# A hybrid attention layer on one core: the softmax division of chunked attention moved to the last stage

## What is computed

```python
def chunk_relbias_attention(q, k, v, rel_bias):
    ...
    scores = scores + bias[None, None]
    ...
    probs = jax.nn.softmax(scores, axis=-1).astype(v.dtype)
    out = jnp.einsum('bnhqk,bnkhd->bnqhd', probs, vb)
...
    ya = ya * jax.nn.silu(ag)
    ...
    mix = jnp.concatenate([ya, yb], axis=-1) @ w_out[i]
    h = DN_ALPHA * x + mix
    h = h + jax.nn.sigmoid(h @ w_ple_gate[i]) * (p[i] @ w_ple_proj[i])
    x = layer_norm(h, ln_g[i], ln_b[i])
```

## Time and profile before

| | us |
|---|---|
| median of 3 runs | 2842.0 |
| lowest and highest | 2839.82, 2842.2 |
| span of the profiled execution | 2843.8 |
| TensorE busy | 2692.4 (95%) |
| VectorE busy | 1398.1 (49%) |
| ScalarE busy | 1192.5 (42%) |
| GpSimd busy | 336.2 (12%) |

### The profile page before, as it was taken

How to read it: one execution, slowest core, us unless ns; L and a number is a source line. 1 busy time by engine, 2 the same in 40 slices (tenths; PEclk the granted TensorE clock), 3 DMA queues, 4 the chain that set the end, 5 groups by cost and what they waited for, 6 DMA issues and landing times.

```text
span 2843.8 us, 40981 instructions
## 1 busy us (share of the span) xinstructions
PE 2692.4 (95%) x14544; PEld 2325.9 (82%) x14544; DVE 1398.1 (49%) x3367; ACT 1192.5 (42%) x2448; POOL 336.2 (12%) x227
## 2 busy tenths in 40 slices
PE   7999999999999999889989898987799999999997
PEld 5888888988888889878888888887688888888886
DVE  5211156232111461589989996778433334333343
ACT  3111122231111221589989997778322222222222
POOL 2000000000000000011111111334112221122211
PEclk9999999999999999999999997778899999999999
DMA  6431246453312463887767647785422211222111
GB/s 196 161 120 63 77 100 148 151 193 126 122 63 77 99 146 111 202 188 160 163 146 161 154 101 163 184 196 145 128 73 72 72 59 61 72 72 72 57 62 54
DMA packets 279246, 339.32 MB, mean 119 GB/s; under 512 B 81712, under 2 KB 201536, under 8 KB 274880
## 3 DMA queue, kind: packets, MB, share of 16 engines
q1 hardware_dynamic: 277648, 335.67, 43.8%
q0 software_dynamic: 1456, 1.86, 0.2%
HBM read 211.10 MB, written 127.41 MB: 119 GB/s over the span
## 4 chain that ended last, share of the span: by engine, by line
PE 71%; DVE 9%; issue 8%; ACT 6%; DMA 5%; POOL 1%; SPq 0%; ACTq 0%; DVEq 0%; POOLq 0%
PE psum L1338 68%; DVE pt_lo L1103 3%; ACT pt_hi L825 2%; ACT prob L807 2%; DMA y_d<-y_b 1%; DMA av<-v_d 1%; DMA x_raw<-in_xT 1%; PE psum L1542 1%; DVE y_a L1151 1%; ACT y_low L816 1%; DVE prob L1137 1%; PE psum L1489 1%; ACT prob L833 1%; POOL y_b L690 1%; ACT prob_b L855 0%
## 5 line engine op out<-in xcount | busy, mean ns | idle before, releaser
L1338 PE MATMUL psum<-x_hi,w_hi 128*128 128x512 f32 x1408 | 549.5, 390 | 20.1 <-DVE x_lo L1008 18.2
L1338 PE MATMUL psum<-x_hi,w_lo 128*128 128x512 f32 x1408 | 549.2, 390 | 0.0
L1338 PE MATMUL psum<-x_lo,w_hi 128*128 128x512 f32 x1408 | 549.1, 390 | 0.0
L1338 PEld LDWEIGHTS psum<-x_hi,w_hi 128*128 128x128 f32 x1408 | 265.3, 188 | 75.6 <-issue 18.2
L1338 PEld LDWEIGHTS psum<-x_lo,w_hi 128*128 128x128 f32 x1408 | 265.2, 188 | 55.3
L1338 PEld LDWEIGHTS psum<-x_hi,w_lo 128*128 128x128 f32 x1408 | 265.1, 188 | 55.1
L683 POOL TENSOR_TENSOR y_a<-y_a,g_a 64x512 f32<-64x512 f32 x64 | 81.4, 1272 | 1582.6 <-DVE y_a L1151 1582.6
L1338 PE MATMUL psum<-wo_hi,y_hi 128*128 128x512 f32 x512 | 204.8, 400 | 15.5 <-DVE y_lo L1241 10.0
L1404 PE MATMUL psum<-ident,prob 128*128 128x128 f32 x1200 | 182.4, 282 | 38.8 <-DVE pt_lo L1103 33.1
L1115 DVE CUSTOM_DVE_ANT_0 prob<-psum,bias 128x640 f32<-128x640 f32 (+4 forms) x256 | 198.8, 777 | 32.5 <-issue 30.3
L807 ACT ACTIVATE prob<-prob,small 128x640 f32<-128x640 f32 (+4 forms) x256 | 202.2, 790 | 27.2 <-DVE small L1130 22.4
(11 more groups left out here) (165 smaller groups left out, 5597.0 us busy)
## 6 DMA issues: line engine op xcount, KB each, us to landing
qk_d<-stage_out SPq DMA_DIRECT2D x80, 512.0 KB, 2.8
w_raw<-in_w_in SPq DMA_DIRECT2D x24, 1024.0 KB, 5.6
x_raw<-in_xT SPq DMA_DIRECT2D x32, 512.0 KB, 4.6
g_d<-stage_out SPq DMA_DIRECT2D x64, 256.0 KB, 2.0
bq_d<-stage_out SPq DMA_DIRECT2D x64, 256.0 KB, 4.1
v_d<-stage_out SPq DMA_DIRECT2D x32, 512.0 KB, 2.9
bq<-bq_d SPq DMA_DIRECT2D x64, 256.0 KB, 4.4
y_raw<-y_d SPq DMA_DIRECT2D x32, 512.0 KB, 4.8
```

The costliest lines, as they stand in the source:

```text
L1338: return pe.matmul(dst, lhs, rhs, start=start, stop=stop)
```

## The change

In the chunked stage the probabilities are no longer normalised. The bias pass writes the negative scaled maximum directly, exp leaves the row sums of a head in a_sum, and after a head's last tile VectorE takes 32 reciprocals at once into a_recip. The two halves of the values are kept apart: both pairs of a quad accumulate in one PSUM bank, ScalarE copies all of it (128x512) to y_a, and SP stores the two halves to ya_d. The matmuls of a pair are done in two parts, three key tiles each where there are six, in successive steps (lags 5 and 6). Transposes follow two steps behind the scores (four before), pt_hi two, pt_lo three. pt_hi and pt_lo get four slots, prob has four instead of eight. Gates are no longer read in this stage and GpSimd has nothing to do in it.

At the end TensorE transposes a_recip, ScalarE copies it and SP stores it to ra_d. In the last stage load_tile reads y_two (both halves of A), g_c (the gates of A), r_c (reciprocals, repeated over 64 partitions, in two DMAs), the B half of y_raw and p. GpSimd's y_tile adds the halves, multiplies gate and reciprocal, and multiplies both into y_raw. y_tile_hi waits for that (y_ready). x is loaded into the slot of h itself; SP issues it ahead of load_tile, once the store of that slot has landed. Two DMAs of the bias table move from GpSimd's to SP's queue. In the diff below, long removed blocks and index changes are left out.

```diff
-VECTOR_NORMS = (1, 3, 5)
 QSLOTS = 4
-RING = 8
+RING = 4
+PT_SLOTS = 4
 A_TURN = 2 * NT
-A_DRAIN = 10
+A_QUADS = A_TURN // 4
+A_DRAIN = 8
...
+        ya_d = scratch("ya_d", [A_HEADS // 2, 2, 2, HEAD, SEQ])
+        yb_d = scratch("yb_d", [D_B, SEQ])
+        ra_d = scratch("ra_d", [A_HEADS // 2, 2, SEQ])
...
-                        sp.wait_ge(y_gated, quad0 + q + 1)
-                        sp.dma_start(y_d[bass.ds(head * HEAD, HEAD), q * TB:q * TB + TB], y_a[:, q % QSLOTS, :]
...
+                        sp.wait_ge(y_copied, quad0 + q + 1)
+                        for c in range(2):
+                            sp.dma_start(ya_d[bass.ds(it, 1), c, s, :, q * TB:q * TB + TB]
+                                         .rearrange("a d t -> (a d) t"),
+                                         y_a[c * HEAD:c * HEAD + HEAD, q % QSLOTS, :]).then_inc(y_stored[q % QSLOTS], 16)
...
+            sp.wait_ge(recipT_copied, 1)
+            sp.dma_start(ra_d.rearrange("a h (t q) -> (a h t) q", q=P).rearrange("(b j) q -> j b q", j=P), recip_t[:, :, :]
+                         ).then_inc(recip_stored, 16)
...
             def load_tile(t, s):
-                sp.dma_start(y_raw[:, s, :, :], y_d[:, bass.ds(t * P, P)].rearrange("(k p) t -> p k t", p=P)
+                cols = bass.ds(t * P, P)
+                sp.dma_start(y_two[:, s, :, :], ya_d[:, :, :, :, cols].rearrange("k c h d t -> (h d) (k c) t")
+                             ).then_inc(y_two_loaded[s], 16)
+                sp.dma_start(g_c[:, s, :, :], g_d[0:D_A, cols].rearrange("(k p) t -> p k t", p=P)
+                             ).then_inc(g_loaded[s], 16)
+                sp.wait_ge(g_scaled, t)
+                for hd in range(2):
+                    sp.dma_start(r_c[hd * HEAD:hd * HEAD + HEAD, :, :],
+                                 ra_d[:, hd, cols].unsqueeze(0).to_broadcast([HEAD, KT // 2, P])).then_inc(r_loaded, 16)
+                sp.dma_start(y_raw[:, s, KT // 2:KT, :], yb_d[:, cols].rearrange("(k p) t -> p k t", p=P)
                              ).then_inc(y_loaded[s], 16)
+                if not isinstance(t, int):
+                    load_p(t, s)
+            def load_p(t, s):
                 sp.dma_start(p_raw[:, s, :, :], pT[:, bass.ds(t * P, P)].rearrange("(k p) t -> p k t", p=P)
                              ).then_inc(p_loaded[s], 16)
-            def load_x(t):
-                sp.dma_start(x_nat[:, :], x[bass.ds(t * P, P), :]).then_inc(xn_loaded, 16)
+            def load_x(t, slot):
+                sp.dma_start(h[slot][:, :], x[bass.ds(t * P, P), :]).then_inc(xn_loaded, 16)
...
-            def stage_c(t, i, more=True):
+            def stage_c(t, i, stored, more=True):
+                slot = (i + 1) % 3
+                if stored is not None:
+                    sp.wait_ge(out_stored[slot], stored + 16)
+                load_x(t + 1, slot)
                 if more:
                     sp.wait_ge(p_split, t + 1)
                     load_tile(t + 2, i % 2)
-                sp.wait_ge(h_done, t + 1)
-                load_x(t + 1)
                 store_out(t, i % 3)
...
-            with pool.Fori(0, QUADS * A_HEADS // QSLOTS) as it:
-                for s in range(QSLOTS):
...
+            def y_tile(t, s, first=False):
+                two = y_two[:, s, :, :].rearrange("p (k c) t -> p k c t", c=2)
+                pool.wait_ge(y_two_loaded[s], 8 * (t - s) + 16)
+                if not first:
+                    pool.wait_ge(y_split, t - 1)
+                pool.tensor_tensor(y_raw[:, s, 0:KT // 2, :], two[:, :, 0, :], two[:, :, 1, :], ALU.add).then_inc(y_joined, 1)
+                pool.wait_ge(g_loaded[s], 8 * (t - s) + 16)
+                pool.wait_ge(r_loaded, 32 * t + 32)
+                pool.tensor_tensor(g_c[:, s, :, :], g_c[:, s, :, :], r_c[:, :, :], ALU.mult).then_inc(g_scaled, 1)
+                pool.wait_ge(y_joined, t + 1)
+                pool.wait_ge(g_scaled, t + 1)
+                pool.tensor_tensor(y_raw[:, s, 0:KT // 2, :], y_raw[:, s, 0:KT // 2, :], g_c[:, s, :, :], ALU.mult
+                                   ).then_inc(y_ready, 1)
...
+            y_tile(0, 0, True)
+            y_tile(1, 1, True)
+            pool.wait_ge(ln_loaded, 32)
+            with pool.Fori(0, 5) as it:
+                for i in range(6):
+                    y_tile(6 * it + i + 2, i % 2)
+                    scale_shift(6 * it + i, i % 3)
...
-                unit = a_unit(it, i, 1)
+                unit = a_unit(it, i, 7)
+                if unit and unit[2] % 4 == 3:
+                    quad = (i - 7) // 4
+                    slot = quad % QSLOTS
+                    act.wait_ge(values_done, A_QUADS * it + quad + 1)
+                    act.wait_ge(y_stored[slot], 32 * (A_QUADS // QSLOTS * it + quad // QSLOTS + 1))
+                    act.activation(y_a[:, slot, :], psum[:, 6 + quad % 2, :], ACT.Copy).then_inc(y_copied, 1)
+                unit = a_unit(it, i, 0)
                 if unit:
                     u, s, t = unit
                     n, r = min(BAND, t + 1), t % RING
-                    act.wait_ge(shift_ready, u + 1)
+                    act.wait_ge(scores_used, u + 2)
+                    if t == 0 and not (isinstance(it, int) and it == 0):
+                        act.wait_ge(recip_ready, 2 * it + s - 1)
                     act.activation(prob[:, r, NBW - n * P:NBW], prob[:, r, NBW - n * P:NBW], ACT.Exp,
-                                   bias=a_col(A_SHIFT, r), scale=SCALE, accum_out=a_col(A_SUM, r)).then_inc(exp_done, 1)
-                unit = a_unit(it, i, 8)
...
+                                   bias=a_low(r), scale=-1.0, accum_out=a_sum[:, s, t:t + 1]).then_inc(exp_done, 1)
+                unit = a_unit(it, i, 2)
...
-                unit = a_unit(it, i, 3)
-                if unit and unit[2] % 8 not in VECTOR_NORMS:
...
+            act.wait_ge(recipT_done, 1)
+            act.activation(recip_t[:, :, :].rearrange("p b q -> p (b q)"), psum[:, 0, 0:2 * P], ACT.Copy
+                           ).then_inc(recipT_copied, 1)
...
+                act.wait_ge(y_ready, t + 1)
...
+                        scale=-SCALE, scalar=3e38, op0=ALU.add, op1=ALU.min,
+                        accum_out=a_low(r)).then_inc(scores_used, 1)
+                unit = a_unit(it, i, 3)
                 if unit:
                     u, s, t = unit
-                    dve.wait_ge(exp_done, u + 1)
-                    dve.reciprocal(a_col(A_RECIP, t % RING), a_col(A_SUM, t % RING)).then_inc(recip_ready, 1)
...
+                    n, e = min(BAND, t + 1), t % 2
+                    dve.wait_ge(probsT_hi, u + 1)
+                    if isinstance(it, int) and it == 0 and u == 6:
                         dve.wait_ge(p_over, 1)
-                    if pr % 2 == 0:
...
+                    at = (slice(None), (t // 2) % PT_SLOTS, slice(e + BAND - n, e + BAND), slice(e * P, e * P + P))
+                    src = psum[:, 2 + 2 * e:4 + 2 * e, :].rearrange("p a b -> p (a b)")[:, 0:n * P]
+                    dve.tensor_tensor(pt_lo[at], src.rearrange("p (j q) -> p j q", q=P), pt_hi[at].bitcast(f32),
+                                      ALU.subtract).then_inc(probsT_split, 1)
+                    if t == NT - 1:
+                        dve.wait_ge(exp_done, u + 1)
+                        dve.reciprocal(a_recip[:, bass.ds((2 * it + s if i - 3 >= 0 else 2 * it - 1) * NT, NT)],
+                                       a_sum[:, s, :]).then_inc(recip_ready, 1)
...
-            def a_values(u, pair, s, pr):
-                pe.wait_ge(probsT_split, u + 3)
-                pe.wait_ge(y_summed, pair + 1)
+            def a_values(u, it, quad, s, pr, part):
                 first_tile = 2 * pr - (BAND - 1)
-                order = [i for i in range(1, BAND) if first_tile + i >= 0]
-                order += [i for i in (0, BAND) if first_tile + i >= 0]
-                for m, i in enumerate(order):
+                order = [i for i in (1, 2, 0, 3, 4, 5) if first_tile + i >= 0]
+                half = (len(order) + 1) // 2
+                bank = psum[:, 6 + pr // 2 % 2, :]
+                if part == 0:
+                    pe.wait_ge(probsT_split, u + 3)
+                    if pr % 2 == 0 and not (isinstance(it, int) and it == 0 and quad < 2):
+                        pe.wait_ge(y_copied, A_QUADS * it + quad - 1)
+                for m in range(0, half) if part == 0 else range(half, len(order)):
+                    i = order[m]
                     c0, c1 = (0, P) if i == 0 else (P, 2 * P) if i == BAND else (0, 2 * P)
+                    at = pr % 2 * 2 * P
                     for pt in (pt_hi, pt_lo):
-                        last = mm(psum[:, 6 + pr % 2, c0:c1], av[:, s, first_tile + i, :], pt[:, pr % 2, i, c0:c1],
+                        last = mm(bank[:, at + c0:at + c1], av[:, s, first_tile + i, :], pt[:, pr % PT_SLOTS, i, c0:c1],
                                   m == 0 and pt is pt_hi, m == len(order) - 1 and pt is pt_lo)
```

(20 more changed lines are left out.)

197 lines of the change are left out of this document (69 added, 128 removed).

## The result

The changed kernel takes 3035.65 us, median of 4 runs (3032.68 to 3044.23), against 2842.1 us (2839.82 to 2845.37) in the same session: 1.068 of the time before, 95% interval 1.066 to 1.070. That is 194 us slower. The prediction said slower, by 80 us, with 2985 us as its upper end.

What follows compares the result with a forecast made beforehand. Bounds: ScalarE, VectorE close behind, in the chunked stage; TensorE in the last, hiding a y-load chain with 1.69 us slack. Sum: 2843.8 - 69 (chunked stage) + 10 (entry) + 139 (last-stage rounds) - 1.8 (profile over median) = 2922 us; range 2850 to 2985.

Steps and rivals of the forecast that it cites:

- rounds: Last stage: the later y tile lengthens each round from 25.4 to 30.2 us, 29 rounds, 139 us lost (26 to 194).
- chunked stage: Chunked stage: a pair of query tiles goes from 4.29 to 3.8 us; the stage gains 69 us together.
- entry: Entry to the last stage: y_tile(0) stands behind GpSimd's last gate product; costs 10 us, bounds 5 and 15.
- when r_c is in place: Last stage's load burst: 2.10 MB up to r_c at 313 GB/s, through at 2324.7, landed at 2325.9.
- The upper bound: Last stage, highest case: 512-byte rows at some 200 GB/s, +1.5, and the whole 0.9 for clock; 6.7 a round, 194 us.
- The estimate from the Trainium skill: Last stage's loads at 2.0 us plus bytes at 436 GB/s: r_c at 2324.0, round about 28.3, total some 55 us lower.
- The clock: Last stage: TensorE's idling slows eight transposes by about 0.9 us; half of that taken, making the round 30.2 us.
- rival 2: Last stage: TensorE's clock stays low, at 0.74 the work of 25.4 us takes 34.3; total 3041, chance 0.05.
- The slack of 1.69 us: Last stage before the change: the chain through store, y load and residual takes 23.7 of 25.4 us, 1.69 to spare.
- Rival 1: Last stage: the y chain stays hidden beside TensorE's work; time 2783, chance 0.10, of which 0.08 faster by over 0.2%.
- ScalarE ends last: Chunked stage before the change: ScalarE's work takes 4.14 of a pair's 4.29 us, VectorE close behind, TensorE's 3.67.
- one bound: Chunked stage, lower bound of the gain: seven heads saving 5 us each, 35 us.

Runs made afterwards that it cites:

- The distinct rows: Changed kernel with both r_c loads reading 64 different rows of g_d each instead of one row of ra_d 64 times; 2958.46 us, ratio 1.041.
- no r_c: Changed kernel without the r_c loads from tile 2 on, old values in r_c used again; 2914.49 us, ratio 1.026.
- slack kernel: Kernel before with independent GpSimd products added between scale and shift: one (128x512) 2845.64 us; two (128x1024, 128x256) 2886.11 us, the one with the 1.76 us idle.

## Why the prediction was wrong

The sign, the mechanism and its place held; the size did not. The forecast was 2922, and by its own terms the difference is: rounds +113 us (252 for 139), chunked stage -11 (80 for 69), sliding-window stage +6 (0 forecast), entry +5 (15 for 10). 2922 + 113 - 11 + 6 + 5 = 3035.

**The failed step: when r_c is in place.** "Up to r_c it is 2.10 MB, through at 2324.7, landed at 2325.9" took every byte at the 313 GB/s of the earlier trace rows. That rate was measured on loads that read each row once, and it held for y_two (6.84 us for 7.0). r_c reads each row 64 times, and its product came at 12.01 us behind the out store for a forecast of 8.7: 3.3 us a round of the 3.9 by which the round was missed (34.08 for 30.2). The distinct rows show that 2.2 of them are the repeats (9.83 us). The other 1.1 are the plain load's, later than the rate said: in the round shown its burst falls to 120 to 210 GB/s in its last part, and I had let one stretch of 5.4 us stand for a burst of 2.1 MB. The upper bound was wrong too: it put short rows at 200 GB/s, +1.5 us (the 1.04 MB of y_two, g_c and r_c come to 1.9 at that rate), and no row of the kernel before shows a repeated source row, so nothing in its bounds stood for that. The estimate from the Trainium skill ("DMA: Bandwidth & Descriptors", section "Anatomy of one DMA") is further off on the same side: its 2324.0 is 6.8 us behind the out store's issue, the runs show 12.0. That section gives its fit per DMA and for the path of GpSimd; the prediction put it to a burst from SP's queue, so this says nothing against the fit itself.

**The clock.** I took half of 0.9 us; all of it came in the round shown (1.97 us for eight transposes), 0.89 on the mean of the step from transposes to scale. That is +0.4 us, 13 us in 30 rounds. The rule of the Trainium skill ("TensorE: Matmul & The Clock Gate", section "Why this matters for your kernels"), that idle gaps between bursts drop the array to half clock, agrees with these rows for 5.25 to 7.64 us of idling. With 2.62 us (no r_c) and 1.76 us (slack kernel) the transposes kept 1.09 us; between 3.00 and 4.65 us they did so in some rounds only. As rival 2, the clock alone for the whole stage, it fell: its time of 3041 was nearly met, but the windows show clock 0.50 only behind the wait (2530 to 2535) and 1.00 again from 2538 to 2550, and 30 x 8.4 us come from the chain.

**What held.** The slack of 1.69 us (extra products: 1.7). The chain behind the r_c load: the g_c product to the next transposes takes 6.55 us. The entry's GpSimd order: three operations stand behind the last gate product, and its 15 us reach the bound given. Rival 1, the hidden chain, was priced at 2783 us; with the loads ahead of the store it is real and took 2781.86. That run also tests the other terms in sum. The rival's place was right: the order of SP's queue decides it, not GpSimd's work.

**The chunked stage, right for a partly wrong reason.** A pair takes 3.63 us for 3.8 predicted: nothing is left over from waits, it is the 3.67 of TensorE's own work. But "ScalarE ends last" was only half of what held the kernel before. The rows gave both numbers, 1.76 for the score bank and TensorE's own parts; I didn't add them for the unspread order, 1.76 + 2.53 = 4.29, which was the pair to the hundredth. ScalarE's 4.14 fitted the same 4.29 less well. The result of the sum is the same, as the change lifts both.

Some of the fit is luck, and one bound was added up wrongly: with the pair at 4.0 us a head saves 68.8 - 56.0 - 5.8 = 7 us, not 5, so seven heads 49 and not 35. A head takes 59.3 us for the 59.0 forecast, but its 14 pairs are 2.4 us shorter and its short tiles with the hand-over take 8.5 us for 5.8. And the 11 us above the forecast are mostly not in the pairs: head 1's scores start at 1231.65 for 1238.98, 7.3 us earlier, where nothing was forecast. 3.5 of these are there at the stage's first scores (1162.44 for 1165.99) and are scatter: the two slack kernels have these scores at 1162.06 and 1163.51. The rest is the first head, which took 69.2 us for 73.0.

**The 6 us of the sliding-window stage** are partly the seams: between profiles of kernels whose code is the same up to there, this stage started between 1650.4 and 1658.1 us, so single stages are known to some 4 us. TensorE was busy 228.4 us in it, before 222.2 for the same 1408 matmuls, at granted clock 0.72 for 0.74. In the kernel with loads ahead it was 212.9 at 0.79. The length goes with the granted clock, which differs from profile to profile; what sets it there is open.

## What to carry to other kernels

A load issued behind a store that waits for the round's end is on the critical path as soon as its consumers grow: read the slack of that chain from one round, and if the new work exceeds it, move the issue one round ahead before adding the work. A burst's rate in GB/s holds only for loads of the same source pattern; a broadcast that re-reads one short DRAM row needs a price of its own, or a few copies of the row. Where two engines both come near the measured period, add up each step's own maximum (bank chain or engine work) before naming one of them the limit.
